# Gates of a recurrent layer multiplied between the two chunks of memory keys

## The reference

```python
proj = h @ w_in                      # 1024 -> 512 (u), 512 (gate), 512 (xq)
u, gate, xq = jnp.split(proj, [D_LRU, 2 * D_LRU], axis=-1)
u = conv(u) + conv_b                 # causal, width 4, per channel
r = sigmoid(blockwise(u, w_r) + b_r);  i = sigmoid(blockwise(u, w_i) + b_i)
log_a = -8 * r * softplus(-lam);       a = exp(log_a)
b = sqrt(-expm1(2 * log_a)) * (i * u)
hs = scan(a, b)                      # h[t] = a[t] * h[t-1] + b[t]
y = hs * gelu(gate)                  # 512 of the 1024 columns before w_out
k, v = split(rms_norm(mem) @ w_kv)   # 256 tokens, 4 heads of 128
o = softmax(norm(xq) @ norm(k).T / sqrt(128)) @ v    # the other 512 columns
x = x + concat(y, o) @ w_out;  x = x + mlp(norm(x))
```

## Time and profile before

| | |
|---|---|
| median of 3 runs | 2482.35 us (2479.43 to 2487.03) |
| profiled execution | 2481.47 us, its span 2479.7 us |
| busy share of the span | PE 94%, PEld 77%, POOL 67%, DVE 42%, ACT 20% |
| layer R, last tile of `h` to first result of `out_proj` | 1338 to 1448 us of the span |

### The profile page before, as it was taken

The page is one execution under the profiler, slowest core; times in us unless marked ns, Lnnn a source line. Parts: engine busy times, 40 slices in busy tenths (PEclk is TensorE's granted clock), DMA queues, the critical chain, the costliest instruction groups (busy, mean ns, idle before and its releaser), DMA issues.

```text
span 2479.7 us, 29722 instructions
## 1 busy us (share of the span) xinstructions
PE 2331.0 (94%) x11040; PEld 1901.3 (77%) x11040; DVE 1051.8 (42%) x1342; ACT 501.6 (20%) x955; POOL 1661.9 (67%) x1370
## 2 busy tenths in 40 slices
PE   5968999999996899999999699999999898999999
PEld 4766788888876678888887468888888776888887
DVE  7664533322366344332237545215334333540430
ACT  3245211110134521111012521001111263100000
POOL 5466677767756667777777577767766564776774
PEclk9988999999998899999999899999999999999999
DMA  4300122222330012222232112222232200222222
GB/s 145 107 27 18 68 102 95 91 87 93 117 107 18 18 69 102 97 89 87 94 124 102 52 68 88 99 102 96 91 119 86 86 35 17 85 102 102 85 102 85
DMA packets 37844, 207.93 MB, mean 84 GB/s; under 512 B 3532, under 2 KB 10316, under 8 KB 16888
## 3 DMA queue, kind: packets, MB, share of 16 engines
q1 hardware_dynamic: 37752, 206.70, 23.9%
HBM read 204.55 MB, written 2.13 MB: 83 GB/s over the span
## 4 chain that ended last, share of the span: by engine, by line
PE 60%; DVE 2%; POOL 2%; ACT 2%; issue 1%; DVEq 0%; POOLq 0%; ACTq 0%
PE ps L821 18%; PE ps L826 18%; PE ps L825 18%; POOL wl L649 1%; PE ps L1185 1%; PE ps L1159 1%; ACT rt L1335 1%; POOL wh L643 0%; PE ps L1160 0%; PE ps L1163 0%; PE ps L1161 0%; DVE sq L1705 0%; DVE t L1713 0%; DVE nt L1705 0%; PE ps L1200 0%
## 5 line engine op out<-in xcount | busy, mean ns | idle before, releaser
L649 POOL TENSOR_TENSOR wl<-raw,wh 128x512 fp32r<-128x512 f32 (+1 forms) x776 | 1032.8, 1361 | 0.0
L643 POOL TENSOR_SCALAR wh<-raw 128x1024 fp32r<-128x1024 f32 (+1 forms) x388 | 427.3, 1121 | 595.3 <-PE ps L821 462.6
L821 PE MATMUL ps<-h,wh 128*128 128x512 f32 x1576 | 618.1, 392 | 18.4 <-POOL wl L649 9.2
L825 PE MATMUL ps<-h,wh 128*128 128x512 f32 x1576 | 615.2, 390 | 0.0
L826 PE MATMUL ps<-h,wl 128*128 128x512 f32 x1576 | 615.1, 390 | 0.0
L821 PE MATMUL ps<-act,wh 128*128 128x512 f32 x1120 | 437.6, 391 | 1.1 <-DVE x L1705 1.1
L825 PE MATMUL ps<-act,wh 128*128 128x512 f32 x1120 | 436.0, 389 | 0.0
L826 PE MATMUL ps<-act,wl 128*128 128x512 f32 x1120 | 436.0, 389 | 0.0
L821 PEld LDWEIGHTS ps<-h,wh 128*128 128x128 f32 x1576 | 297.0, 188 | 85.5 <-issue 24.4
L825 PEld LDWEIGHTS ps<-h,wh 128*128 128x128 f32 x1576 | 296.9, 188 | 62.3 <-issue 1.0
L826 PEld LDWEIGHTS ps<-h,wl 128*128 128x128 f32 x1576 | 297.0, 188 | 62.1
(11 more groups left out here) (337 smaller groups left out, 2681.8 us busy)
## 6 DMA issues: line engine op xcount, KB each, us to landing
raw<-w_gu SPq DMA_DIRECT2D x44, 1024.0 KB, 4.8
raw<-w_up SPq DMA_DIRECT2D x32, 1024.0 KB, 4.8
raw<-w_down_b SPq DMA_DIRECT2D x32, 1024.0 KB, 4.8
raw<-w_down_a SPq DMA_DIRECT2D x32, 704.0 KB, 4.0
raw<-w_in_a SPq DMA_DIRECT2D x14, 1024.0 KB, 4.9
raw<-w_in_f SPq DMA_DIRECT2D x13, 1024.0 KB, 4.8
raw<-w_in_r SPq DMA_DIRECT2D x11, 1024.0 KB, 4.8
raw<-w_out_a SPq DMA_DIRECT2D x8, 1024.0 KB, 7.6
```

The costliest lines, as they stand in the source:

```text
L643: pool.tensor_scalar(hi_s[:, part], raw[s][:, part], 1.0, 1.0, ALU.mult, ALU.mult).then_inc(hi_done, 1)
L649: ins = pool.tensor_tensor(lo_s[:, part], raw[s][:, part], hi_s[:, part].bitcast(F32), ALU.subtract)
L821: first = pe.matmul(out, w_hi, v_hi, start=start, stop=False)
L825: pe.matmul(out, w_hi, v_lo, start=False, stop=False)
```

## The change

The second chunk of memory keys is stored behind the gate chunk, and PE takes the gates between the two chunks of keys: the keys become tiles 12, 13, 22 and 23, the gates 14 to 21. On ACT the gelu, the sigmoids, tanh and exp come ahead of the squares of `rxk` and of `stat(5)`. The callback `then`, which `mem_in` runs ahead of its second chunk, is `gates` here. A recurrence writes its scan over `uc` and its product over `rg`, and keeps no `sq` buffer; POOL waits for it by a semaphore of its own and reads `rg`. Recurrences 0 and 1 are done by DVE in the loop of the memory values, behind the second and the fourth tile; recurrences 2 and 3 in iterations 0 and 1 of the heads.

```diff
+MEM_TILES_R, GATE_TILE, MEM_TILES_F = (12, 13, 22, 23), 14, (21, 22, 23, 24)
@@ POOL, attention
                     if recurrence and hd < 4:
-                        mixed(slice(0, P), hd)
+                        pool.wait_ge(rec_ready, hd + 1)
+                        mixed(slice(0, P), hd, rg[:, hd, :])
@@ PE, mem_in
-                        tt = t0 + 2 * c + j
+                        tt = tiles[2 * c + j]
@@ PE, new
+            def gates():
+                s = chunk()
+                for j in range(4):
+                    pe.wait_ge(uc_ready, ucr.up())
+                    for gate in range(2):
+                        tt = GATE_TILE + 2 * j + gate
+                        bb = claim(tt)
+                        done(passes(ps[bb][:, :], wh[s][:, 4 * gate + j, :], wl[s][:, 4 * gate + j, :],
+                                    uch[:, j, 0, :], uch[:, j, 1, :], True, True), tt)
@@ PE, in_r
-                mem_in(12, 4, 0)
+                mem_in(MEM_TILES_R, 4, 0, gates)
                 mem_gathers(4)
-                s = chunk()
...
-                        tt = 16 + 2 * j + gate
...
@@ ACT, in_r
                 stat(4, 0, full, P, 1.0)
-                for i in range(4):
-                    sc.wait_ge(free[i], bk.emptied(i, 3))
-                    square(4 + i, full, rxk[:, i, :], M_MEM)
-                stat(5, 0, full, M_MEM // TB, 1.0)
                 for i in range(4):
                     fn(rg[:, i, :], rg[:, i, :], ACT.Gelu_apprx_tanh).then_inc(gelu_ready, 1)
...
                     fn(ra[:, j, :], ra[:, j, :], ACT.Exp, scale=csn[:, j:j + 1]).then_inc(act_step, 1)
                     step.up()
                 sc.wait_ge(act_step, step.at())
+                for i, tt in enumerate(MEM_TILES_R):
+                    sc.wait_ge(free[tt % 4], bk.emptied(tt % 4, tt // 4))
+                    square(4 + i, full, rxk[:, i, :], M_MEM)
+                stat(5, 0, full, M_MEM // TB, 1.0)
                 prep(XA, 0)
@@ DVE
-            def mixed_out():
+            def mixed_out(back=1):
                 if mixo.n >= 2:
-                    dve.wait_ge(mixed_ready, mixs.at(-1))
+                    dve.wait_ge(mixed_ready, mixs.at(-back))
...
                 for i in range(4):
                     mem_values(24, rxv, i)
+                    if i % 2:
+                        recurrence(i // 2)
@@ DVE, recurrence
-                w, hs = nt[:, 0, :], nt[:, 1, :]
+                w, hs = t[:, 2, :], uc[:, i, :]
...
-                dst = mixed_out()
-                tt(dst, hs, rg[:, i, :], ALU.mult, mixo)
+                tt(rg[:, i, :], hs, rg[:, i, :], ALU.mult, recd)
@@ DVE, attention, output of a head
-                    dst = mixed_out()
+                    dst = mixed_out((3 if hd < 3 else 2) if m.name == "xa" and layers[l] == "R" else 1)
@@ DVE, attention, end of an iteration
                     if m.name == "xa" and layers[l] == "R" and hd < 4:
-                        recurrence(hd)
+                        mixs.n += 1
+                        if hd < 2:
+                            recurrence(2 + hd)
@@ order of the stored weights
-    return [blocks(w[:, 0:512]), wide(w[:, 512:768]), wide(w[:, 768:1024])]
+    return [blocks(w[:, 0:256]), blocks(w[:, 256:512]), wide(w[:, 512:768]), wide(w[:, 768:1024])]
```

More of the change, by code:

```diff
@@ L457, in build @@
         max_ready, dg_ready, mix_out = sem("max_ready"), sem("dg_ready"), sem("mix_out")
+        rec_ready = sem("rec_ready")
         up_ready = sem("up_ready")
@@ L982, in pooled, with mem_in @@
                        dpool[:, i, 1, :], True, True).then_inc(ready[7], 1)
-            def mem_in(t0, n0, gu, then=None):
+            def mem_in(tiles, n0, gu, then=None):
                 pe.wait_ge(mem_ready, mr.up(KT))
@@ L1026, in in_r @@
                     gathered(2, i, slice(0, P), 4, i, i == 0, i == 3)
-                mem_in(12, 4, 0)
+                mem_in(MEM_TILES_R, 4, 0, gates)
                 mem_gathers(4)
-                s = chunk()
-                for j in range(4):
-                    pe.wait_ge(uc_ready, ucr.up())
-                    for gate in range(2):
-                        tt = 16 + 2 * j + gate
-                        bb = claim(tt)
-                        done(passes(ps[bb][:, :], wh[s][:, 4 * gate + j, :], wl[s][:, 4 * gate + j, :],
-                                    uch[:, j, 0, :], uch[:, j, 1, :], True, True), tt)
                 bk.close(EARLY_IN)
@@ L1072, in in_f @@
                     gathered(2, i, slice(0, P), 4, 8 + i, i == 0, i == 3)
-                mem_in(21, 12, 1, lambda: (bk.close(EARLY_IN), start(FOX)))
+                mem_in(MEM_TILES_F, 12, 1, lambda: (bk.close(EARLY_IN), start(FOX)))
                 mem_values(25)
@@ L1493, in in_r @@
                     for gate, bias, dst in ((1, "ib", ru), (0, "rb", ra)):
-                        tt = 16 + 2 * j + gate
+                        tt = GATE_TILE + 2 * j + gate
                         sc.wait_ge(ready[tt % 4], bk.filled(tt % 4, tt // 4))
                         fn(dst[:, j, :], ps[tt % 4][:, :], ACT.Sigmoid, bias=col(bias, j)).then_inc(free[tt % 4], 1)
-                sc.wait_ge(free[2], bk.emptied(2, 5))
+                sc.wait_ge(free[(GATE_TILE + 6) % 4], bk.emptied((GATE_TILE + 6) % 4, (GATE_TILE + 6) // 4))
                 for j in range(4):
@@ L1698, in _ @@
             gel = Count(gelu_ready, kept)
+            recd = Count(rec_ready, kept)
             sqrtr = Count(sqrt_ready, kept)
@@ L1927, in mem_out, with mem_keys @@
                 stat(6, 1, full, 2, 1.0 / D, rtokm)
-            def mem_keys(t0, xk, scale):
-                for i in range(4):
-                    b, u = (t0 + i) % 4, (t0 + i) // 4
+            def mem_keys(tiles, xk, scale):
+                for i, tt_i in enumerate(tiles):
+                    b, u = tt_i % 4, tt_i // 4
                     dve.wait_ge(ready[b], bk.filled(b, u))
@@ L1954, in in_r @@
                 head_stat(4, 0, T, 1)
-                mem_keys(12, rxk, t[:, 1, :])
+                mem_keys(MEM_TILES_R, rxk, t[:, 1, :])
                 head_stat(5, 0, M_MEM, 1, 64)
@@ L2025, in in_f @@
                 start(FOX, 3)
-                mem_keys(21, fxk, fe)
+                mem_keys(MEM_TILES_F, fxk, fe)
                 for i in range(4):
```

## The result

The changed kernel takes 2487.83 us (median of 20 runs, 2482.51 to 2489.05), the kernel before 2482.12 us (20 runs). The ratio is 1.0019, 95% interval 1.0013 to 1.0025, so 3 to 6 us slower (the two medians lie 5.7 apart, the ratio stands for 4.7). The forecast was 2486 us with +4.4 in the sum. The profiled execution's span is 2486.3 us.

The account below looks back on a forecast made before the run. The prediction took PE's waits in layer R's memory stage and attention, on POOL, ACT and DVE, as the bound. It summed 4.9 + 3.7 - 1.0 - 5.2 + 2.0 = +4.4 us to 2486 us, range 2479 to 2491.5.

Parts of the forecast that it names:

- Step 1: Gates and key-head statistics in layer R's memory stage: late row sums make PE start the values 4.9 us late (0.6 to 6.2).
- rival (a): Memory stage: statistics not late, values start before 1372.5, so not slower, sum +0.1 or -0.7, 2481 us; chance 0.2.
- Step 2: Memory values: recurrence 0 covered by POOL's split and free, recurrence 1 uncovered ahead of the first maxima, costing 3.7 us.
- Step 3: Head iterations 0 and 1: contention adds 1.0 us; POOL's first output chunk starts at 1419.0, 7.6 late.
- Step 4: End of the attention: POOL's chain with a first chunk of 7.8 us gives 5.2 us back (3.4 to 6.0).
- The last term: End of the attention: PE, some 6 us ahead, sits idle before head 2's tile and loses 2.0 us of clock (0 to 2.6).
- the signs that were named: Layer R's trace: two loads around Ln, recurrence order, first chunk near 1419 under 8.5 us, PE idle ahead of head 2's tile.
- Rival (c): Layer R: all terms at their dear ends, with late values and contended recurrences, +10.2 us or 2491.5; chance 0.2.
- (b): First half of the attention at full PE clock, gaining 2.5 us, and no clock loss at the end: 2476 us; chance 0.05.
- (d): Memory values: sqrt late, both recurrences ahead of the first maxima, up to 4.1 us more, 2490; chance 0.05.

Follow-up runs that it names:

- second pair: Second profiles of the unchanged kernel before and of the changed kernel, set against each other; layer R 5.1 us longer after the change.
- whole_again: The whole changed kernel, nothing further altered, measured and profiled once more against the kernel before; ratio 1.0023 (1.0014 to 1.0033).
- named_set: The changed kernel plus one table set holding both Ln and Exp, loaded by name ahead of the gates' exp; 1.0017 of the kernel before.
- gates_only: The changed kernel's order of gates and statistics, but all four recurrences, in place, in iterations 0 to 3 of the heads; 1.0029 of the kernel before.
- one_early: The changed kernel with only recurrence 0 beside the values, and recurrences 1, 2 and 3 in iterations 0, 1 and 2; 1.0031 of the kernel before.
- first pair: First profiles of the kernel before and of the changed kernel, set against each other; layer R 4.1 us longer after the change.
- stats_first: The changed kernel with the Ln and Exp set loaded by name, and key squares and statistics ahead of the gates' exp; 1.0002 of the kernel before.

## Why the prediction was right, step by step

Step 1 held. The values began 5.3 us late (6.3 in the second pair, just over the bound of 6.2) where 4.9 were forecast. The two loads came as taken, and cost 2.6, not 2.2; the 0.4 behind the sums wasn't there. The sigmoids ended 19.5 us from the first key matmul, between the bounds of 18.1 and 21.1 and 0.7 sooner than the value taken; PE's granted clock over the first six gate matmuls was 0.53 in that profile and 1.00 in whole_again. The argument against rival (a), that each gap of PE had cost it clock, doesn't hold in the trace of the kernel before: behind the wait of 1.64 us at 1379.27 it was granted 1.00.

The 2.66 us a switch of the Trainium skill ("ScalarE: Activation LUTs", "What ACT_TABLE_LOAD costs") isn't what this trace has: each switch was the load of 1.28 and nothing beside it. Its rule to group functions by table set ("Table sets: the hidden batching unit") agrees with the runs: in named_set exp, Ln and Exp share one set, and the two added loads and 2.6 us are gone.

Step 2 held: recurrence 0 was covered, recurrence 1 wasn't. From the end of the values to the first maxima it is 5.0 us, 1.0 before, so 4.0 against 3.7; another 0.2 lie in the values, which ran at a granted clock of 0.53 for their first 4 us, mostly under the cover of POOL's split. Step 3 was 1.5 short. The tile of recurrence 1 took 3.2 beside the end of recurrence 3, not 2.05, and the key work of head 3 was 1.2 later beside the recurrences, where 1.0 was taken. POOL's first chunk was 9.9 late, not 7.6. Step 4 gave back 5.8 instead of 5.2, since the chunk took 7.0 where 7.8 was taken.

The last term, 2.0 for PE's clock, was wrong. It took PE to be 6 us ahead of POOL; PE's own turn through the heads ended only 1.7 ahead, and no clock was lost. The mechanism is there, but in other runs: 2.7 in gates_only, 2.2 in one_early. The +4.4 are 4.9 + 3.7 - 1.0 - 5.2 + 2.0; measured in the first pair are 5.25 + 4.22 + 0.45 - 5.84 + 0.02 = 4.10, in the second 6.32 + 4.16 + 0.46 - 5.89 + 0.01 = 5.06. The account of the loss, late statistics and an uncovered recurrence against a faster end of the attention, is what the runs show. That the sum came out so near is partly luck: steps 1, 2 and 3 were short by 2.3 together, step 4 and the clock term too dear by 2.6.

Of the signs that were named, both loads, the order of the recurrences and the short chunk (7.0, named as under 8.5) came. The chunk began at 1421.3 with the 3.0 taken off, where 1419 was named, and PE idled 1.7 us ahead of head 2's tile instead of some us.

Two figures of the working need a correction. With its own cheap bounds (step 3's contention at 0 too) the sum goes down to -3.7, so the low end is 2477.8 and not 2479. And the 0.3% that it took for the least that can be told from no change is too much here: 20 runs of each kernel tell 0.19% from nothing. Of the rivals, (a) didn't happen, and stats_first shows what it would have been: with the statistics in time the kernel takes 2481.3 us, beside 2481.4 for the kernel before, where (a) gave 2481. Rival (c) had the right sign and too much contention, (b) and (d) didn't occur. The part that the runs leave open is whether the early recurrences alone win the 0.9 us that their trace shows.

## What to carry to other kernels

When a step is moved behind others on one engine, read what its last result opens: here a small statistic on ACT, moved behind exp, held PE's next 96 matmuls, and it brought two table loads because the set loaded for exp didn't serve Ln. Idle time of GpSimd beside VectorE's recurrences is not free: a chunk of 7.0 us takes 9.4 to 10.1 there and the recurrences grow with it (from 4.1 up to 8.4), so place such work where VectorE waits. And below 0.3% compare positions inside the stage, with two profiles of each kernel, before a term of 2 us is believed.

## What the runs showed of the hardware that I had not expected

One and the same program has a stretch at a granted clock of 0.77 in one profile and 1.00 in the next, after the same wait of 2.38 us. By the next chunk this is worth 1.2 us, and the two profiles end layer R 2.1 apart. Ahead of head 2's tile a wait of 5.93 us cost PE half its rate for the next twelve matmuls (2.7 us) and one of 4.25 cost 2.2; waits of 1.68 and 2.96 at the same place cost nothing.
